# Gate and up products of the feed-forward layer by seven block products for eight

## What is computed

```python
h = rmsnorm_2(x, g_pre_ffn[l]) * (1.0 + sc_f) + sh_f
f = (jax.nn.silu(h @ w_gate[l]) * (h @ w_up[l])) @ w_down[l]   # 2048 -> 5632 -> 2048
x = x + gt_f * rmsnorm_2(f, g_post_ffn[l])
```

## Time and profile before

| | us |
|---|---|
| median of 3 runs | 3206.47 |
| lowest, highest | 3204.05, 3208.24 |
| span of the profiled execution | 3201.8 |
| TensorE busy in it | 3156.7 |
| VectorE, ScalarE, GpSimd busy in it | 1723.7, 916.3, 268.9 |

### The profile page before, as it was taken

How to read it: one execution, slowest core, us unless ns; L and a number is a source line. 1 busy time by engine, 2 the same in 40 slices (tenths; PEclk the granted TensorE clock), 3 DMA queues, 4 the chain that set the end, 5 groups by cost and what they waited for, 6 DMA issues and landing times.

```text
span 3201.8 us, 38265 instructions
## 1 busy us (share of the span) xinstructions
PE 3156.7 (99%) x14744; PEld 2603.3 (81%) x14744; DVE 1723.7 (54%) x2260; ACT 916.3 (29%) x1124; POOL 268.9 (8%) x414
## 2 busy tenths in 40 slices
PE   8999999999999999999998999999999999999998
PEld 7888877888878888888777888888888888888887
DVE  6666665868874445556788643333333333323354
ACT  5333343223233333444522221111121121121213
POOL 1111100111100000000013220000000000000013
PEclk9999999999999999999998999999999999999999
DMA  5444455766742222222564642322322223222354
GB/s 185 142 132 133 127 187 215 289 255 230 259 190 79 84 87 79 80 79 79 225 251 169 240 133 92 111 93 100 110 92 101 102 98 105 98 98 102 124 179 163
DMA packets 93449, 455.83 MB, mean 142 GB/s; under 512 B 19744, under 2 KB 20016, under 8 KB 56112
## 3 DMA queue, kind: packets, MB, share of 16 engines
q1 hardware_dynamic: 51776, 298.08, 26.4%
q0 software_dynamic: 37696, 128.52, 11.2%
q10 hardware_dynamic: 3888, 28.03, 2.3%
HBM read 421.81 MB, written 26.22 MB: 140 GB/s over the span
## 4 chain that ended last, share of the span: by engine, by line
PE 96%; DVE 3%; DMA 0%; ACT 0%; DVEq 0%; issue 0%; SPq 0%; ACTq 0%
PE PS L1076 24%; PE PS L1078 24%; PE PS L1077 24%; PE PS L1478 5%; PE PS L1477 5%; PE PS L1476 5%; PE PS L1345 1%; PE PS L1372 1%; PE PS L1129 1%; PE PS L1130 1%; PE PS L1131 1%; PE PS L1360 1%; PE PS L1242 0%; PE PS L1201 0%; DVE WL L1523 0%; PE PS L1224 0%
## 5 line engine op out<-in xcount | busy, mean ns | idle before, releaser
L1076 PE MATMUL PS<-XH,WH 128*128 128x512 f32 x3312 | 1298.0, 392 | 5.8 <-DVE WL L1523 2.8
L1078 PE MATMUL PS<-XH,WL 128*128 128x512 f32 x3312 | 1289.0, 389 | 0.0
L1077 PE MATMUL PS<-XL,WH 128*128 128x512 f32 x3312 | 1288.8, 389 | 0.0
L1523 DVE TENSOR_TENSOR WL<-RAW,WH 128x2048 fp32r<-128x2048 f32 x266 | 609.5, 2292 | 498.8 <-ACT WH L680 498.7
L680 ACT ACTIVATE WH<-RAW 128x2048 fp32r<-128x2048 f32 x266 | 509.0, 1914 | 1242.8 <-PE PS L1078 875.4
L1076 PEld LDWEIGHTS PS<-XH,WH 128*128 128x128 f32 x3312 | 621.7, 188 | 145.8 <-issue 13.5
L1078 PEld LDWEIGHTS PS<-XH,WL 128*128 128x128 f32 x3312 | 621.7, 188 | 130.1
L1077 PEld LDWEIGHTS PS<-XL,WH 128*128 128x128 f32 x3312 | 621.8, 188 | 129.6 <-issue 2.2
L1476 PE MATMUL PS<-WH,FH 128*128 128x512 f32 x704 | 273.9, 389 | 0.0
L1477 PE MATMUL PS<-WL,FH 128*128 128x512 f32 x704 | 273.9, 389 | 0.0
L1478 PE MATMUL PS<-WH,FL 128*128 128x512 f32 x704 | 273.9, 389 | 0.0
(11 more groups left out here) (320 smaller groups left out, 2299.9 us busy)
## 6 DMA issues: line engine op xcount, KB each, us to landing
RAW<-w_units_dram SPq DMA_DIRECT2D x268, 1024.0 KB, 4.8
ADA<-w_ada_dram POOLq DMA_DIRECT2D x192, 512.0 KB, 5.5
spill_dram<-SIG POOLq DMA_DIRECT2D x24, 256.0 KB, 2.3
BB<-x_t_dram ACTq DMA_DIRECT2D x1, 4096.0 KB, 15.8
x_dram<-RES ACTq DMA_DIRECT2D x1, 4096.0 KB, 14.9
BB<-x_dram ACTq DMA_DIRECT2D x4, 1024.0 KB, 7.9
x_dram<-BB ACTq DMA_DIRECT2D x4, 1024.0 KB, 5.1
X3T<-x3t_dram ACTq DMA_DIRECT2D x4, 1024.0 KB, 4.9
```

The costliest lines, as they stand in the source:

```text
L1076: pe.matmul(PS[:, bank, :], wh, rh[:, x, :], start=k == 0, stop=False)
L1077: pe.matmul(PS[:, bank, :], wh, rl[:, x, :], start=False, stop=False)
L1078: ins = pe.matmul(PS[:, bank, :], wl, rh[:, x, :], start=False, stop=k == n - 1)
L1523: v.tensor_tensor(WL[:, slot, :], RAW[:, slot, :], f32(WH[:, slot, :]), ALU.subtract)\
```

## The change

After two plain pairs, 42 pairs are computed with seven block products in place of eight. The inner dimension (2048) is cut in two halves and the tokens in two halves of 256; gate and up weights are the two row blocks. Each product multiplies a sum of weight blocks (128x1024) with a sum of data blocks (1024 x 256). The data sums are made once, before the phase, and stand in TA, TB and TC with high and low part side by side: one matmul of 512 columns multiplies the high weights with both, one of 256 columns the low weights with the high data; they add up in one PSUM bank. The weight sums are made for each pair by four adds on GpSimd (SUM3, SUM2 and two in place). ScalarE rounds the seven weight operands, VectorE takes their low parts, and VectorE combines the products into gate and up tiles in a staging area ST in the freed half of XH and XL. The hidden tile goes to DRAM (f_d). The down product is a second phase over all 44 tiles, with the hidden tiles read back in chunks of four and split again; adaLN chunks and transposes move to this phase. A pair's weights (2 MB) are loaded into one of two buffers.

```diff
+PLAIN = 2
+FAST = FF_TILES - PLAIN
+LOOPED = FAST - 2
+O_DOWN = O_FFN + 2 * PLAIN
...
+PRODUCTS = 7
+HALF_S = S // 2
+FULL_K = DT // 2
+NEED_SUM = {1: 1, 2: 2, 4: 3, 6: 4}
+NEED_T = {1: 2, 2: 1, 4: 4, 5: 3}
...
+    ST = at("ST", X0, [P, 2, DT, S])
+    TA = at("TA", B0 + 32 * K, [P, 2, FULL_K, S], FP32R)
+    TB = at("TB", B0, [P, FULL_K, S], FP32R)
+    TC = at("TC", B0 + 16 * K, [P, FULL_K, S], FP32R)
+    FO = [TMP, at("FO1", 64 * K, [P, S])]
+    DS = SM1[:, 40:48]
+    ST_P1, ST_V, ST_G, ST_U, ST_GATE, ST_UP = 0, 1, 2, 4, 6, 7
...
+        g, u, h = RAWS[s2][:, 0, :], RAWS[s2][:, 1, :], FULL_K * P
+        return [g[:, 0:h], SUM3[:, :], u[:, 0:h], g[:, h:2 * h], SUM2[:, :], u[:, h:2 * h], g[:, h:2 * h]][j]
...
+            with sp.Fori(0, LOOPED // 4) as i:
+                for e in range(4):
+                    for k in (1, 0):
+                        sp.wait_ge(q_lo, 28 * i + (Q0 + PRODUCTS * e + 7 - k))
+                        sp.dma_start(RAWS[e % 2][:, k, :], w_units[bass.ds(8 * i + (U_FFN + 2 * PLAIN + 2 * e + 4 + k), 1)]
+                                     .rearrange("a p n -> p (a n)")).then_inc(pair_loaded[e % 2], 16)
+                    hidden_saved(4 * i + (e + 1), f_d[bass.ds(4 * i + (e + 1), 1)].rearrange("a p n -> p (a n)"),
+                                 (e + 1) % 2)
...
+            def weight_sums(s, r, n):
+                g, u, h = RAWS[r][:, 0, :], RAWS[r][:, 1, :], FULL_K * P
+                gp.wait_ge(pair_loaded[r], n)
+                gp.wait_ge(q_lo, PRODUCTS * s + (Q0 - PRODUCTS + 2))
+                gp.tensor_tensor(SUM3[:, :], g[:, 0:h], u[:, 0:h], ALU.add).then_inc(sum_ready, 1)
+                gp.drain()
+                gp.tensor_tensor(u[:, 0:h], u[:, 0:h], u[:, h:2 * h], ALU.add).then_inc(sum_ready, 1)
+                gp.drain()
+                gp.wait_ge(f_made, PLAIN)
+                gp.wait_ge(q_lo, PRODUCTS * s + (Q0 - PRODUCTS + 5))
+                gp.tensor_tensor(SUM2[:, :], SUM3[:, :], u[:, h:2 * h], ALU.add).then_inc(sum_ready, 1)
+                gp.drain()
+                gp.wait_ge(q_lo, PRODUCTS * s + (Q0 + 4))
+                gp.tensor_tensor(g[:, h:2 * h], g[:, h:2 * h], SUM2[:, :], ALU.add).then_inc(sum_ready, 1)
...
+            def hi_part(s, s2, j, slot, done):
+                act.wait_ge(q_done, done)
+                if j in NEED_SUM:
+                    act.wait_ge(sum_ready, 4 * s + NEED_SUM[j])
+                act.activation(QH[:, slot, :], weight(s2, j), ACT.Copy).then_inc(q_hi, 1)
...
+            def gated(s):
+                act.wait_ge(gate_summed, s + 2)
+                act.activation(staged(ST_GATE), staged(ST_GATE), ACT.Silu).then_inc(silu_done, 1)
+            def fast_pair(s, e, loaded, more=True):
+                s2, n2 = e % 2, (e + 1) % 2
+                q = PRODUCTS * s + Q0
+                for j in range(2, PRODUCTS):
+                    if j + 3 < PRODUCTS:
+                        hi_part(s, s2, j + 3, (PRODUCTS * e + j + 3) % 4, q + j)
+                    elif more:
+                        if j + 3 == PRODUCTS:
+                            act.wait_ge(pair_loaded[n2], loaded)
+                        hi_part(s + 1, n2, j - 4, (PRODUCTS * e + j + 3) % 4, q + j)
+                    if j == 2:
+                        act.wait_ge(up_summed, s + 1)
+                        half_copied(ST_U + 1, 7 - 4 * s2, q + 2)
+                    if j == 4:
+                        act.wait_ge(gate_summed, s + 1)
+                        half_copied(ST_G, 4 - 4 * s2, q + 4)
+                if more:
+                    hi_part(s + 1, n2, 3, (PRODUCTS * e + PRODUCTS + 3) % 4, q + PRODUCTS)
+                    gated(s)
+                    p1_copied(s + 1, n2)
+                    hi_part(s + 1, n2, 4, (PRODUCTS * e + PRODUCTS + 4) % 4, q + PRODUCTS + 1)
...
+            plain_silu(0)
+            third_hi(act, U_FFN + 2, 2, 1)
+            act.wait_ge(saved, 80)
+            act.wait_ge(t_sum, 1)
+            act.activation(TA[:, 0, :, 0:HALF_S], RES[:, 0:FULL_K, 0:HALF_S], ACT.Copy).then_inc(t_hi, 1)
+            act.wait_ge(out_done, O_FFN + 2)
+            prep_hi(U_FFN // 2 + 1, 1)
+            act.wait_ge(t_sum, 2)
+            for t in range(FULL_K):
+                ins = act.activation(TA[:, 1, t, 0:HALF_S], RES[:, t, HALF_S:S], ACT.Identity, bias=DS[:, t:t + 1])
+            ins.then_inc(t_hi, 1)
+            act.wait_ge(t_sum, 4)
+            act.wait_ge(t_lo, 2)
+            act.activation(TB[:, :, 0:HALF_S], RES[:, FULL_K:DT, 0:HALF_S], ACT.Copy).then_inc(t_hi, 1)
+            plain_silu(1)
+            act.wait_ge(pair_loaded[0], 32)
+            for j in range(2):
+                hi_part(0, 0, j, j, 1)
+            act.wait_ge(t_lo, 3)
+            for t in range(FULL_K):
+                b = 3 * DT + FULL_K + t
+                ins = act.activation(TC[:, t, 0:HALF_S], RES[:, FULL_K + t, HALF_S:S], ACT.Identity,
+                                     bias=MOD[:, b:b + 1])
+            ins.then_inc(t_hi, 1)
+            act.wait_ge(out_done, O_FFN + 2 * PLAIN)
+            hi_part(0, 0, 2, 2, 1)
+            hi_part(0, 0, 3, 3, 1)
+            p1_copied(0, 0)
+            hi_part(0, 0, 4, 0, Q0 + 1)
...
+            def fast_data(j, k):
+                lo = slice(0, HALF_S)
+                return [XHL[:, :, k, lo], in_halves(TA[:, 1, k, :]), in_halves(TA[:, 0, k, :]),
+                        XHL[:, :, FULL_K + k, lo], in_halves(TC[:, k, :]), in_halves(TB[:, k, :]),
+                        XHL[:, :, FULL_K + k, HALF_S:S]][j]
+            def fast_pair(s, e):
+                b0 = 4 - 4 * (e % 2)
+                q = PRODUCTS * s + Q0
+                for j in range(PRODUCTS):
+                    slot = (PRODUCTS * e + j) % 4
+                    bank = b0 + (0, 3, 2, 0, 1, 3, 2)[j]
+                    pe.wait_ge(q_lo, q + j + 1)
+                    if j in NEED_T:
+                        pe.wait_ge(t_lo, NEED_T[j])
+                    if j == 0:
+                        pe.wait_ge(copied, 3 * s + (COPIED0 - 3))
+                    elif j == 3:
+                        pe.wait_ge(copied, 3 * s + (COPIED0 + 1))
+                    elif j == 5:
+                        pe.wait_ge(copied, 3 * s + (COPIED0 + 2))
+                    else:
+                        pe.wait_ge(taken, 4 * s + (TAKEN0 + {1: -5, 2: -4, 4: -6, 6: 1}[j]))
+                    for k in range(FULL_K):
+                        wh, wl = (w[:, slot, k * P:(k + 1) * P] for w in (QH, QL))
+                        x = fast_data(j, k)
+                        pe.matmul(in_halves(PS[:, bank, :]), wh, x, start=k == 0 and j not in (3, 5, 6), stop=False,
+                                  skip_group_check=True)
+                        ins = pe.matmul(PS[:, bank, 0:HALF_S], wl, x[:, 0, :], start=False, stop=k == FULL_K - 1,
+                                        skip_group_check=True)
+                    ins.then_inc(q_done, 1)
...
+            def lo_part(s, s2, j, slot):
+                v.wait_ge(q_hi, PRODUCTS * s + (j + 1))
+                v.tensor_tensor(QL[:, slot, :], weight(s2, j), f32(QH[:, slot, :]), ALU.subtract).then_inc(q_lo, 1)
+            def both(i):
+                return (ST[:, a, i:i + 2, HALF_S:S] for a in range(2))
+            def fast_pair(s, e, saved, more=True):
+                s2, n2, b0 = e % 2, (e + 1) % 2, 4 - 4 * (e % 2)
+                q = PRODUCTS * s + Q0
+                r = staged(ST_U + 1)
+                def bank(i):
+                    return in_halves(PS[:, b0 + i, :])
+                for j in range(2, PRODUCTS):
+                    if j + 3 < PRODUCTS:
+                        lo_part(s, s2, j + 3, (PRODUCTS * e + j + 3) % 4)
+                    elif more:
+                        lo_part(s + 1, n2, j - 4, (PRODUCTS * e + j + 3) % 4)
+                    if j == 3:
+                        v.wait_ge(copied, 3 * s + (COPIED0 + 2))
+                        v.wait_ge(q_done, q + 3)
+                        v.tensor_tensor(r, r, bank(2), ALU.subtract).then_inc(taken, 1)
+                    if j == 5:
+                        v.wait_ge(q_done, q + 5)
+                        v.tensor_tensor(staged(ST_V), bank(1), staged(ST_P1), ALU.subtract).then_inc(taken, 1)
                         v.drain()
-
-                        v.wait_ge(out_done, o + k + 1)
-                        if k % 2 == 0:
-                            continue
-                        j = k // 2
-                        if first and j == 0:
-
-                            v.wait_ge(saved, 80)
-                        v.wait_ge(sig_ready, 24 + FF_CHUNK * c + j + 1)
-
-                        v.tensor_tensor(FV[:, :], PS[:, k % 4, :], SIG[:, j % 2, :], ALU.mult).then_inc(out_read, 2)
-                        v.drain()
-                        v.tensor_copy(FH[:, j, :], FV[:, :]).then_inc(sig_used, 1)
-                        v.drain()
```

(112 more changed lines are left out.)

382 lines of the change are left out of this document (240 added, 142 removed).

## The result

The changed kernel takes 3219.14 us (median of 4 runs, 3217.75 to 3220.28), the kernel before 3205.81 beside it (4 runs): ratio 1.0044, 95% interval 1.0030 to 1.0058. The forecast was 3217, slightly slower, range 3155 to 3265. It held, and so did its mechanism: VectorE and the port that it shares with GpSimd set the pace of the new loop.

A forecast was written before the change was run, and what follows sets the result against it. TensorE bounds the kernel before, VectorE and its shared port the new loop. Pairs -8.9, start +7, clock +2, border +8.6, clock +2: +10.7 us on the 3201.8 span, 3212.5; plus 4.7 from span to median, 3217; range 3155 to 3265.

The forecast's parts named there:

- The add of 1024: GpSimd's weight-sum add of 128x1024, a size never measured: 2.38 us, between 1.27 and 2.54.
- The hold: Time one GpSimd add keeps the port shared with VectorE: 2.20 us, bounds 1.09 and 2.36.
- The burst: After product 3's low part, all four GpSimd adds come together and delay VectorE's two-SBUF-input operations; final product ends at 12.05.
- The pair: One gate/up pair in the fast phase takes VectorE 21.6 us, against 21.76 before; the last pair 19.4.
- TensorE's own pair: A pair if TensorE stayed the bound: 56 x (0.2267 + 0.120) = 19.42 us, saving 98 us over 42.
- rival 1: Fast phase: adds cost less than priced, TensorE stays the bound, pairs 19.42, 3128 us; chance 0.20 with in-between values.
- TensorE's waits: In the fast phase TensorE waits about 2.1 us per pair, before products 4 and 5.
- Start and border: TensorE idles 7 us at the fast phase's start (2.5 to 12) and 8.6 before the down phase (6 to 12).
- Clock: Half pace after each of the two idle stretches, at start and border: 2 us each (0 to 3).
- rival 2: Fast phase: weight load not hidden behind 256 columns, short matmul 0.19, pairs 23.3, 3290 us; chance 0.09.
- Rival 4: The change does not do what it says, not giving 4704 + 2112 matmuls; chance 0.03 with the rest.
- rival 3: Fast phase: waits before products 4 and 5 repeatedly lower the clock, some 3 us per pair, about 3335; chance 0.04.

The follow-up runs named there:

- add3_twice: The changed kernel with GpSimd's third add per pair done twice in a row, same result; 3323.38 us, ratio 1.0372 to the kernel before.
- adds_4: The changed kernel with its four GpSimd adds per pair cut to 4 of 1024 columns, waits kept; 3135.95 us, ratio 0.9781 to the kernel before.
- early_down: The changed kernel with the first four hidden tiles and down unit 0 rounded during the last pair; 3216.18 us, ratio 1.0033 to the kernel before.
- v_adds: The changed kernel with the four weight sums per pair on VectorE instead of GpSimd, spread over its list; 3147.8 us, ratio 0.9821 to the kernel before.
- combined: The changed kernel with sums on VectorE, product 0's copy ahead of the SiLU, start, border and loads reordered; 3125.91 us, ratio 0.9755 to the kernel before.
- grouped: combined with each product's eight 512-column matmuls first, then its eight of 256, instead of alternating; 3120.02 us, ratio 0.9737 to the kernel before.

## Why the prediction was right

Each step of it against the changed kernel's trace:

- **The add of 1024.** Priced 2.38; 2.39 to 2.40 alone, 2.66 to 2.86 where it met VectorE. The size that no row of before showed was the weak term, and the upper end (nearly proportional) was the right choice. The estimate for this size that the prediction worked out from the figure of the Trainium skill, "GPSIMD Engine Reference", section 3.1 (4497 ns for 2048), is 2.34 to 2.35, 2 to 3% below the measured 2.40.
- **The hold.** Priced 2.20. The add at L585 ends at 2211.63, low part 4, which alone takes 1.22, at 2212.72: the port came free about 0.13 before the recorded end of the add. By add3_twice one more add costs a pair 2.2. The rule of the Trainium skill, "SBUF — State Buffer", section "SBUF: two separate sides", that the loser blocks for the whole instruction, is nearly what these rows show; with 4 x 0.18 more per pair it would have given about 3247, and the measured pair excludes that.
- **The burst.** Predicted ends after low part 3: gate sum 3.0, up sum 5.8, low part 4 9.1, final product 12.05, low part 5 13.2, the next low part 3 21.5 to 21.6. From the rows above (low part 3 ends at 2203.51): 3.0, 5.9, 9.2, 12.2, 13.4, 21.7. The order of engines, read from the code, with four durations was enough to place each within 0.2 us.
- **The pair.** Predicted 21.6; measured 21.68 (median; the mean from the third on is 21.70). 41 pairs by 0.1 are 4 us. The first two took 22.6 and 22.8, 2 us more, which is the half clock at the start, priced at 2. The last took 19.8, not 19.4.
- **TensorE's own pair.** Estimated 19.42 with 0.120 for the short matmul and 0.2267 for the long one. The short one is 0.117, at the lower bound of the earlier trace rows; the long one is not the 0.2267 of the earlier trace rows but 0.230 to 0.236 among short ones. 19.41 or 19.79 came out. This didn't bear on the forecast, as VectorE was the bound, but it is why adds_4 came to 3136 and not 3125, and it makes rival 1's 3128 too low.
- **TensorE's waits.** Predicted 2.1 per pair before products 4 and 5; measured 0.69 and 1.27 (means of what the starts are apart beyond the usual 0.117), together 2.0.
- **Start and border.** 7 predicted for the start, 7.0 in the waits; 8.6 predicted for the border, 8.6 in the waits. Both were sums over in-order lists, and adds_4 shows the adds' part in the start: 2.7 instead of 7.0.
- **Clock.** Half clock at either end, as the windows show; 2 us lost in the first two pairs and 2 in the down phase (480.7 us instead of 2112 x 0.2267 = 478.8). 2 and 2 were predicted.
- **The sum and its luck.** +10.7 on the span was predicted, +16.8 came. Of the 6.1 between them 4 are the pace of the pairs, 0.4 the last pair, 0.3 start and border, and 1.2 the part ahead of the phase (its last matmul starts at 1801.0 and not 1799.8). That last part is within what executions differ by: in early_down, whose work up to there is the same, that matmul starts at 1798.9. Between the medians it is +13.3. The other term was wrong: 4.7 between span and median of the runs was to carry over, and it is 3219.14 - 3218.6 = 0.5. In the runs listed a time is about 1.7 above its own span, so the profiled execution of before was one of about 3203.5, quicker than its three timed runs; the profiled one of the changed kernel (3220.28) is the slowest of its four. So the time is 2 us from the forecast because 6 too little in the span and 4 too much in this term nearly cancel: that closeness is luck, the pace of the pairs is not.

The rivals: rival 2 is out, by 0.117 for the short matmul with a weight load record of 0.189 (median) beside it. Rival 4 is out by the counts (4704 + 2112). Rival 1 fell by 0.5 us in the length of an add, and rival 3 did not happen at waits of 1.4 but at 3.3. What the forecast's closeness to no change hides is that two big terms nearly cancel, and both were some 10 to 15 us too large: 98 us of TensorE time saved and 89 given back at the port were predicted. With pairs of 19.79, as in adds_4, 83 are saved, and the port gives back 41 x 1.9 = 78. As VectorE's list sets the pair in either case, the error fell out of the forecast. v_adds, combined and grouped, 58, 77 and 84 us faster than the kernel before beside them, show that the saving is to be had.

## What to carry to other kernels

Work moved to a helper engine that shares a port with a busy one is not free: price it by the port time that it takes from the busy engine, and compare that with doing the work there (here 2.2 against 1.14 us per add). It costs nothing only as long as the busy engine has slack: here up to adds of some 1.9 us, and beyond that the whole excess. When arithmetic is taken away from the bounding engine, write out the in-order list of the next one for a single period before believing in the gain. An idle stretch at a stage border covers loads queued later; shorten it and look at the next two units.
